# Depthwise convolution of 31 taps: seven taps from TensorE to VectorE, the last tile's chunks earlier, the diagonals in sixteen pieces

## The reference

```
def conformer_conv(h, w_pw1, b_pw1, w_dw, b_dw, ln_g, ln_b, w_pw2, b_pw2):
    u = h @ w_pw1 + b_pw1
    a, gate = jnp.split(u, 2, axis=-1)
    u = a * jax.nn.sigmoid(gate)
    u = causal_dwconv_2(u, w_dw, b_dw)          # 31 taps, one filter per feature
    u = jax.nn.silu(layernorm(u, ln_g, ln_b))
    return u @ w_pw2 + b_pw2
```

## Time and profile before

| quantity | value |
|---|---|
| median of three runs | 1091.67 us |
| the profiled execution | 1091.13 us |
| its span | 1089.3 us |
| PE busy | 1059.7 us, 97% |
| DVE busy | 732.4 us, 67% |
| ACT busy | 529.6 us, 49% |
| POOL busy | 150.0 us, 14% |
| mean granted clock of TensorE | 0.991 of full speed |

### The profile page before, as it was taken

One profiled execution on the slowest core, in us unless ns is written; L12 is line 12 of the kernel. 1 busy time (PEld: TensorE's weight loads), 2 busy tenths in 40 slices (PEclk: granted clock), 3 DMA queues, 4 the chain that ended last, 5 costly groups with the idle time before them and its releaser, 6 DMA issues. The chain is left out here.

```text
span 1089.3 us, 22563 instructions
## 1 busy us (share of the span) xinstructions
PE 1059.7 (97%) x8623; PEld 1001.0 (92%) x8623; DVE 732.4 (67%) x1148; ACT 529.6 (49%) x908; POOL 150.0 (14%) x190
## 2 busy tenths in 40 slices
PE   9999889899999999998999999999999999999998
PEld 8999669699999999876999999999986699999998
DVE  5876667565557765333777677777967677767775
ACT  6453555554444346335644444465735555444442
POOL 0060020011114310002000100031014500010000
PEclk9999999899999999999999999999998999999999
DMA  9563206256565564650565555646730035555551
GB/s 338 162 189 93 95 20 194 68 165 189 180 183 167 169 213 121 199 174 8 174 197 190 182 184 176 192 144 184 235 132 22 2 122 187 194 183 183 178 193 55
DMA packets 51042, 169.86 MB, mean 156 GB/s; under 512 B 5664, under 2 KB 10784, under 8 KB 50848
## 3 DMA queue, kind: packets, MB, share of 16 engines
q1 hardware_dynamic: 45216, 163.22, 46.9%
q10 hardware_dynamic: 5760, 5.70, 1.8%
HBM read 162.16 MB, written 1.05 MB: 150 GB/s over the span
## 5 line engine op out<-in xcount | busy, mean ns | idle before, releaser
L1497 DVE TENSOR_TENSOR WL<-WR,WH 128x1024 fp32r<-128x1024 f32 x302 | 378.1, 1267 | 147.0 <-ACT WH L1236 144.5
L852 PE MATMUL acc<-XH,WH 128*128 128x256 f32 x1392 | 402.0, 289 | 2.8 <-DVE XP L1514 1.7
L853 PE MATMUL acc<-XL,WH 128*128 128x256 f32 x1392 | 393.2, 283 | 0.0
L854 PE MATMUL acc<-XH,WL 128*128 128x256 f32 x1392 | 393.0, 282 | 0.0
L1236 ACT ACTIVATE WH<-WR 128x1024 fp32r<-128x1024 f32 x302 | 312.2, 1051 | 124.9 <-PE acc L854 88.8
L852 PEld LDWEIGHTS acc<-XH,WH 128*128 128x128 f32 x1392 | 265.9, 191 | 6.4 <-DVE WL L1497 2.7
L853 PEld LDWEIGHTS acc<-XL,WH 128*128 128x128 f32 x1392 | 266.1, 191 | 0.9
L854 PEld LDWEIGHTS acc<-XH,WL 128*128 128x128 f32 x1392 | 266.1, 191 | 0.0
L852 PE MATMUL big<-UH,WH 128*128 128x256 f32 x608 | 171.6, 282 | 0.6 <-POOL UL L1954 0.3
L853 PE MATMUL big<-UL,WH 128*128 128x256 f32 x608 | 170.8, 281 | 0.0
L854 PE MATMUL big<-UH,WL 128*128 128x256 f32 x608 | 170.5, 280 | 0.0
(11 more groups left out here) (289 smaller groups left out, 1236.7 us busy)
## 6 DMA issues: line engine op xcount, KB each, us to landing
WR<-weights SPq DMA_DIRECT2D x302, 512.0 KB, 3.6
STK<-UP ACTq DMA_DIRECT2D x32, 142.0 KB, 3.9
X<-x_t SPq DMA_DIRECT2D x4, 256.0 KB, 6.6
MEM<-mem_t SPq DMA_DIRECT2D x1, 1024.0 KB, 10.2
result_t<-X SPq DMA_DIRECT2D x4, 256.0 KB, 2.2
CON<-constants SPq DMA_DIRECT2D x1, 880.0 KB, 13.1
CBUF<-KCV ACTq DMA_DIRECT2D x4, 128.0 KB, 4.9
CBUF<-KCV ACTq DMA_DIRECT2D x4, 127.5 KB, 5.8
```

The source lines that it names most:

```text
L852: pe.matmul(out, wh, hi, start=start, stop=False, skip_group_check=True)
L853: pe.matmul(out, wh, lo, start=False, stop=False, skip_group_check=True)
L854: return pe.matmul(out, wl, hi, start=False, stop=stop, skip_group_check=True)
L1497: dve.tensor_tensor(WL[:, cs % SPL], WR[:, cs % RAW], WH[:, cs % SPL].bitcast(F32), ALU.subtract).then_inc(w_low, 1)
```

## The change

QUADS goes from 8 to 6: PE computes 24 of the 31 taps. The last seven taps (OWN = 7) are computed by DVE out of UP into a new tile CD: one multiplication with the bias added (`tensor_scalar`), then six multiply-adds, each of which waits for the one before. `conv_out` moves from ACT to DVE and becomes an addition of the bank of `big` and CD. The seven taps of tile j - 2 are put around the value half of tile j: four ahead of it and three behind its gating. On PE the two chunks of the last tile come directly behind those of tile 6, ahead of three of the convolutions; on DVE nothing of the convolution stands within the last tile's gate and value halves. GpSimd makes the diagonals in sixteen pieces of 128x384, in turns 8 to 23 of the MLP, where it made eight of 128x1024.

```diff
-QUADS = (CONV_W + 3) // 4
+QUADS = 6
+OWN = CONV_W - 4 * QUADS
...
-                pe.wait_ge(sem("diagonals"), j + 1)
+                pe.wait_ge(sem("diagonals"), 2 * j + 2)
...
             for j in range(KD):
-                if j + 2 < KD:
+                if j < KD - 3:
                     gated(j + 2)
+                if j == KD - 4:
+                    gated(KD - 1)
                 taps(j)
...
-            def conv_out(j):
-                act.wait_ge(sem("taps_ps"), j + 1)
-                act.activation(CX[:, j], big[:, j % 4, 0:T], ACT.Identity, bias=vec("b_dw", j)).then_inc(sem("cx_whole"), 1)
...
-                if j >= 3:
-                    conv_out(j - 3)
-            for j in range(KD - 3, KD):
-                conv_out(j)
...
-            dve.memset(UPAD[:, :, CONV_W - 1 + T:], 0.0)
...
-            for j in range(8):
+            def own_taps(j, first, stop):
+                for n in range(first, stop):
+                    i = 4 * QUADS + n
+                    x, w, o = UPAD[:, j % UPS, i:i + T], vec("w_own", OWN * j + n), CD[:, j % 2]
+                    if n == 0:
+                        dve.wait_ge(sem("up_ready"), j + 1)
+                        link(dve.tensor_scalar(o, x, w, vec("b_dw", j), ALU.mult, ALU.add))
+                    else:
+                        link(dve.scalar_tensor_tensor(o, x, w, o, ALU.mult, ALU.add))
+
+            def conv_out(j):
+                dve.wait_ge(sem("taps_ps"), j + 1)
+                dve.tensor_tensor(CX[:, j], big[:, j % 4, 0:T], CD[:, j % 2], ALU.add).then_inc(sem("cx_whole"), 1)
+
+            for j in range(KD):
                 gate_half(j)
+                if 3 <= j < KD - 1:
+                    conv_out(j - 3)
+                if 2 <= j < KD - 1:
+                    own_taps(j - 2, 0, 4)
                 value_half(j)
                 gated(j)
+                if 2 <= j < KD - 1:
+                    own_taps(j - 2, 4, OWN)
+            for j in range(KD - 4, KD):
+                if j > KD - 4:
+                    own_taps(j, 0, OWN)
+                conv_out(j)
...
-                pool.tensor_tensor(DG[:, j], con("ident4").unsqueeze(1).broadcast_to([P, 4 * QUADS, 32]),
-                                   w.unsqueeze(2).broadcast_to([P, 4 * QUADS, 32]), ALU.mult).then_inc(sem("diagonals"), 1)
+                n = 2 * QUADS
+                w = VEC[:, VCOL["w_dw"] + n * j:VCOL["w_dw"] + n * (j + 1)]
+                pool.tensor_tensor(DG[:, j // 2, n * (j % 2):n * (j % 2) + n], con("ident4").unsqueeze(1).broadcast_to([P, n, 32]),
+                                   w.unsqueeze(2).broadcast_to([P, n, 32]), ALU.mult).then_inc(sem("diagonals"), 1)
...
-                if 18 <= j < 26:
-                    diagonals(j - 18)
+                if 8 <= j < 24:
+                    diagonals(j - 8)
```

More of the change, by code:

```diff
@@ L51 @@
            ("mem_g", 8), ("ff_g", 8), ("final_g", 8), ("mix2_g", 16), ("ffn2_g", 16), ("b_pw1", 16),
-           ("w_dw", 8 * 4 * QUADS), ("b_dw", 8), ("ln_g", 8), ("ln_b", 8), ("b_pw2", 8),
+           ("w_dw", 8 * 4 * QUADS), ("w_own", 8 * OWN), ("b_dw", 8), ("ln_g", 8), ("ln_b", 8), ("b_pw2", 8),
            ("q_g", 1), ("kc_g", 1), ("ks_g", 1), ("kw_g", 1), ("fconv", 2 * UP_TILES * 4),
@@ L166, in program @@
         OS = QT
-        B = group([("SG", [P, 2, T], F32), ("AT", [P, 2, T], F32), ("UP", [P, UPS, STACKED + 4], F32),
-                   ("CX", [P, KD, T], F32), ("MU", [P, T], F32), ("STK", [P, UPS, 4, STACKED], F32),
+        B = group([("SG", [P, 2, T], F32), ("AT", [P, 2, T], F32), ("UP", [P, UPS, T + CONV_W - 1], F32),
+                   ("CX", [P, KD, T], F32), ("MU", [P, T], F32), ("CD", [P, 2, T], F32), ("STK", [P, UPS, 4, STACKED], F32),
                    ("DG", [P, KD, 4 * QUADS, 32], F32)])
-        SG, AT, UPAD, CX, MU, STK, DG = (B[n] for n in ("SG", "AT", "UP", "CX", "MU", "STK", "DG"))
+        SG, AT, UPAD, CX, MU, CD, STK, DG = (B[n] for n in ("SG", "AT", "UP", "CX", "MU", "CD", "STK", "DG"))
         C = group([("GU", [P, 2, T], F32), ("UH", [P, 2, T], F32R), ("UL", [P, 2, T], F32R),
@@ L1938, in diagonals @@
             def diagonals(j):
-                w = VEC[:, VCOL["w_dw"] + 4 * QUADS * j:VCOL["w_dw"] + 4 * QUADS * (j + 1)]
-                pool.tensor_tensor(DG[:, j], con("ident4").unsqueeze(1).broadcast_to([P, 4 * QUADS, 32]),
-                                   w.unsqueeze(2).broadcast_to([P, 4 * QUADS, 32]), ALU.mult).then_inc(sem("diagonals"), 1)
+                n = 2 * QUADS
+                w = VEC[:, VCOL["w_dw"] + n * j:VCOL["w_dw"] + n * (j + 1)]
+                pool.tensor_tensor(DG[:, j // 2, n * (j % 2):n * (j % 2) + n], con("ident4").unsqueeze(1).broadcast_to([P, n, 32]),
+                                   w.unsqueeze(2).broadcast_to([P, n, 32]), ALU.mult).then_inc(sem("diagonals"), 1)
             def scaled_x(name):
@@ L2084, in stacked @@
     def stacked(w):
-        w = np.concatenate([w, np.zeros((4 * QUADS - CONV_W, D), w.dtype)]).reshape(QUADS, 4, 8, 4, 32)
+        w = w[:4 * QUADS].reshape(QUADS, 4, 8, 4, 32)
         return w.transpose(4, 1, 2, 3, 0).reshape(P, -1)
@@ L2102 @@
         "b_pw1": _features(a["conv_b_pw1_2"][0][gate_then_a], 16),
-        "w_dw": stacked(a["conv_w_dw_2"][0]), "b_dw": _features(a["conv_b_dw_2"][0], 8),
+        "w_dw": stacked(a["conv_w_dw_2"][0]), "w_own": taps(a["conv_w_dw_2"][0][4 * QUADS:], 8), "b_dw": _features(a["conv_b_dw_2"][0], 8),
         "ln_g": _features(a["conv_ln_g_2"][0], 8), "ln_b": _features(a["conv_ln_b_2"][0], 8),
```

## The result

The median is 1081.06 us (five runs, 1079.08 to 1084.06), before 1091.67 in the same comparison. The ratio is 0.989, with a 95% interval of 0.987 to 0.992: faster by about 1.1%. The profiled execution took 1081.06 us, its span fell from 1089.3 to 1079.3 us and the mean granted clock from 0.991 to 0.989.

The account below looks back on a forecast made before the run. PE, busy for 97% of the span, was taken as the bound. From 1091.13 us, -3.6 (middle convolutions) - 1.0 (end of stage) - 0.6 (diagonals) + 1.9 (clock) gave 1087.8 us, with a range of 1085.0 to 1090.0.

Parts of the forecast that it names:

- What goes from PE: Convolution stage: each convolution runs 24 of 32 matmuls, 2.69 us instead of 3.59, 7.2 us over eight if nothing becomes late.
- What comes to DVE: Convolution stage: seven taps on DVE at 0.52 us each from start to start, 3.57 us, bounds 0.49 and 0.63 per tap.
- the third rival: Taps cost 0.63 us as in the gated MLP; end chain 2.0 us longer, 1089.8 or 1087.9 us; chance 0.10.
- The end of the stage: Last tiles: DVE's chain sets the end, mean at 25.4 us instead of 26.4, so 1.0 us gained where PE alone gives 3.6.
- The diagonals: MLP ahead of the stage: shorter GpSimd pieces, 0.9 us, end PE's waits for UL; 0.6 us gained.
- The clock: End of stage: two PE waits together lower the granted clock during the sums of squares; 1.9 us lost, up to 3.7.
- The second: Case where the clock stays up at the end of the stage; 1085.9 us, chance 0.30.
- the fourth case: Clock slow from PE's wait in the end chain until pw2 starts; 1093.0 us, chance 0.08 together with long diagonal pieces.
- Chunks and sums stay as they are: PE in the convolution stage: only convolutions get shorter; no change of time counted for chunks and sums.
- What is behind the stage is unchanged.: Work after the convolution stage: no difference counted, 0 us for both gated MLPs.
- The range: Whole kernel: 8 in 10 between 1085.0 and 1090.0 us, from a clock that stays up to the slower taps.

Follow-up runs that it names:

- short_tail: Changed kernel without six of the seven own taps in tiles 5, 6 and 7, so part of the convolution isn't computed; 1076.81 us.
- before_pieces: Kernel before with only the diagonals changed, to sixteen pieces of 128x512 in turns 8 to 23; 1091.57 us.
- u_at_40: Changed kernel with UH and UL put 32 bytes further on, back at their old distance; 1086.23 us, ratio 0.995.
- keep_clock: Changed kernel with 8 idle matmuls in PE's wait ahead of the last sum over features; 1079.91 us, ratio 0.989.
- x_w_at_8: Changed kernel with a pad of 8 bytes ahead of XH, so all tiles move by 8 bytes together; 1079.52 us.
- last_tile_back: Changed kernel with PE's two chunks of the last tile back behind the convolution of tile 4, DVE's order as changed; 1079.13 us.
- before_u_at_8: Kernel before with UH and UL 32 bytes further on, at 8 past a multiple of 64; 1094.6 us, ratio 1.003.
- u448: Changed kernel with 78 columns ahead of UH and 2 behind UL, putting them at remainder 448 by 512 instead of 136; 1094.04 us.
- x_at_8: Changed kernel with XH, XL, YH and YL moved by 8 bytes and the weight tiles by 64; 1070.46 us, ratio 0.983.
- x_at_8_again: The same program as x_at_8 in another execution; 1068.97 us.
- w_at_64: Changed kernel with a pad of 64 bytes ahead of WR alone, moving everything from WR on; 1071.41 us.
- both: Changed kernel with a pad of 64 bytes ahead of WR and 5 idle matmuls ahead of the last sum; 1070.85 us, ratio 0.980.
- before_w_at_64: Kernel before with a pad of 64 bytes ahead of WR and nothing of the change; 1073.09 us in a single execution.
- w64_u168: Changed kernel with WR and all behind 64 bytes further on, UH and UL another 32, and 8 idle matmuls ahead of the last sum; 1063.71 us, ratio 0.975.
- w64_u448: As w64_u168, with UH and UL 312 bytes further on instead of 32; 1065.44 us, ratio 0.976.

## Why the prediction was wrong, step by step

- **What goes from PE: right.** A convolution takes 2.73 us (forecast 2.69), a middle turn 9.10 (9.07), and DVE's wait for PE in it is 1.78 (1.7).
- **What comes to DVE: right.** A tap from start to start is 0.52 us in straight code; the third rival, 0.63, is out.
- **The end of the stage: right.** From the gate eviction of tile 6 to the last gating are 475.90 - 464.00 = 11.9 us to its start and 12.4 to its end (forecast 12.3), and to the mean 25.2 (25.4). DVE's chain has no gap, and `short_tail` shows that it was the bound. The wait ahead of the last sum was 1.87 us where 2.4 were forecast: PE reached it 0.3 us later, and the last sum began sooner behind CX.
- **The diagonals: right in kind, small in size.** The wait of PE for UL is gone. It gave 1.1 us, in `before_pieces` and `u_at_40` alike; the sum had 0.6, the two waits that the profile puts down to UL, where six chunks were 1.1 us longer in all. Two splits take 2.85 us beside a piece where they take 2.4 alone.
- **The clock: the fall right, its reason not, the size too small.** The sums of squares ran at 0.50 and cost 2.6 us, not 1.9, since 5.4 us of the low stretch lay in them and not 3.8. `keep_clock` shows that this cost is the clock's. It lies in the forecast's own range of 1.0 to 3.7 (whose lower end is 1085.9 + 1.0 = 1086.9 us, not 1086.7). But the argument added the two waits up, and the clock fell at 489.16, 0.7 us behind the first wait and ahead of the second. And in `x_w_at_8` it stayed at 1.00 with waits of 0.58, 1.37 and 1.43 us. That it fell was forecast by a sum that doesn't decide it, which is partly luck. The second and the fourth case are out.
- **The step that failed** stands in two sentences: "Chunks and sums stay as they are" and "What is behind the stage is unchanged." The instructions of the chunks are the same, but each down chunk matmul takes 114.1 ns instead of 118.3, 4.3 us less in the two gated MLPs together and 3.2 in the MLP ahead of the stage. The span came out 6.7 us under the forecast: 7.5 from this and 0.5 from the diagonals, less 0.7 for the clock and 0.6 in all the rest. The cause is a side effect of the change: a smaller table moved UH and UL by 32 bytes against the weights. `u_at_40` undoes that alone, and has the old spacing and 1086.23 us. Against the forecast of 1087.8, the rest is small: 1.1 instead of 0.6 from the diagonals, 1.7 us for the clock in that execution, and the 0.9 us that remain are within what runs of one kernel differ by.
- **The range** had bounds for each cost that was thought of, and none for a change of pace in work that the change doesn't touch. PE is busy for 97% of the span, so 1% of its pace is 10 us, more than any term of the sum.

What stays open is the mechanism of the placement: why the distances set the pace, and why a stage can settle at one of two paces. No run here shows either.

## What to carry to other kernels

Where PE is the bound, look whether the change alters the size or order of tiles in SBUF, a table of constants too; if it does, the matmuls behind it may run at another pace, and the range has to hold that. Compare first the starts of matmuls in a stretch that the change leaves alone: it takes a few rows in each kernel and tells whether the pace has changed where no work has. To tell that it is the placement, put the tiles back with a padding, as `u_at_40` does. Once the work is settled, try paddings of the operands and of the weights, in pairs, with more than one execution of each.

## What the runs showed of the hardware

**Spacing by placement.** A matmul of 128x256 with rounded operands, from start to start at a granted clock of 1.00. The distances are from WH to the operand, in bytes, worked out from the order and the sizes of the tiles (XH stands ahead of WH, UH behind it); "up" is XH and XL, "down" is UH and UL; three numbers are the MLP and the two gated ones.

| kernel | XH | UH | up, ns | down, ns |
|---|---|---|---|---|
| before, before_pieces, u_at_40 | 57344 | 52904 | 119.3 to 119.8 | 118.3 |
| after, keep_clock, last_tile_back, short_tail, x_w_at_8 | 57344 | 52872 | 119.2 to 119.6 | 114.1 |
| before_u_at_8 | 57344 | 52936 | 120.0 | 120.0 |
| u448 | 57344 | 53184 | 120.0 | 120.0 |
| x_at_8 | 57400 | 52872 | 113.3, 113.4, 117.7 | the same |
| x_at_8_again | 57400 | 52872 | 113.3, 117.8, 117.8 | the same |
| w_at_64, both | 57408 | 52872 | 113.3, 117.8, 117.8 | the same |
| before_w_at_64, w64_u168 | 57408 | 52904 | 114.7, 114.0, 114.0 | 118.1 |
| w64_u448 | 57408 | 53184 | 114.1, 113.7, 113.7 | 119.2 |

The five kernels of the second row ran in five executions with the same spacings. The pace of the up chunks is not a matter of XH alone (57408 gives 113.3 or 114), nor that of the down chunks of UH alone (52904 gives 118.3 or 118.1, 53184 gives 120.0 or 119.2): X, U and the weights have to be taken together. Between the placements are up to 6%.

**Waits and the clock.** At the end of the stage it fell 0.7 us behind one wait of 1.87 us (after), within one of 2.76 (`last_tile_back`), and behind 0.31, 0.55 and 1.42 (`both`). It stayed at 1.00 with 0.58, 1.37 and 1.43 in `x_w_at_8`, whose window is

```profile
484.00:500.00 16.00, 12.43 (x107) 9.73 (x108) 10.99 (x28) 7.42 (x17) 0.94 (x2) 1.00 0.01 2
```

So neither the longest wait (1.42 us in `both`, 1.43 here) nor their sum (2.3 and 3.4) tells which way it goes. The low stretch was 6.8 us in `after` and 3.4 in `both` and `last_tile_back`.

**A split beside GpSimd.** The split starts 0.2 us behind the piece. With 0.63, 0.85 and 1.71 us of the piece left (`after`, `before_pieces`, before) two splits take 0.45, 0.66 and 1.5 us longer than 2.4: the rest of the piece less some 0.2. The Trainium skill (SBUF — State Buffer, section "Who interferes with whom") says that a VectorE operation with two inputs in SBUF and a GpSimd operation that reads SBUF exclude each other, for the whole instruction; the traces agree with it at three lengths of the piece, up to that 0.2.
